# First gated layer of a three-layer network: 18 of its 22 hidden blocks by seven block products instead of eight

## The chip, the cores and the metric

The kernel runs on one core of one Trainium2 chip. The core has a matrix engine (TensorE, PE in the profile), three engines for elementwise work (VectorE or DVE, ScalarE or ACT, GpSimd or POOL), and SyncE (SP), whose queue issues the loads. Each engine works through its own queue in order, and the queues wait for one another on counting semaphores. The metric is the device time of one execution of the whole kernel, in microseconds (us); less is better.

## The reference

The network has two layers with normalised residuals, each a mixer and a gated feed-forward part, and a third layer of another kind with modulated norms. The part that is changed is the gated part of layer 0, on x of 1024 tokens by 1024 features with 2816 hidden features:

```python
def swiglu(x, w_gate, w_up, w_down):
    return (jax.nn.silu(x @ w_gate) * (x @ w_up)) @ w_down
...
        x = layer_norm(DN_ALPHA * x + swiglu(x, ffn_w_gate[layer], ffn_w_up[layer], ffn_w_down[layer]),
                       ffn_ln_g[layer], ffn_ln_b[layer])
```

Beside it lies a product that belongs to the third layer, 24 rows at a time: silu of a condition times the rows of `w_ada`, one number for each feature (`modulation`).

## The kernel before

**Layout.** Features lie on the 128 partitions: x is eight blocks (`DB`) of 128 features by 1024 tokens (`S`); `HALF` is 512 tokens. Hidden features come in 22 blocks (`FFB`) of 128. A PSUM tile `ps0` to `ps3` holds 128 x 1024 f32, two banks of 512 columns.

**Products in three passes.** Each f32 product is made of three matmuls: every operand is split into a high and a low part, and high x high, high x low and low x high are added up in PSUM. x is split into `xh` and `xl` by the norm before, a hidden block into `hh` and `hl`. A weight unit (128 x 1024 f32, 512 KB) is loaded by SP into one of two buffers `stage`, split by ACT into `whi` (`split_hi`, line 178) and by DVE into `wlo` (`split_lo`, line 185), and then used by PE (`mm_unit`, line 202). The next unit for a buffer is loaded once its split is done.

**The gated stage of layer 0.** The hidden blocks go in three groups, 0 to 7, 8 to 14 and 15 to 21. The first four blocks are done by token halves while the norm before is still at work (`Hidden`, `early_act`, `early_dve`, `early_pe`). All others are pairs of a gate unit and an up unit with 48 matmuls each (8 feature blocks x 3 passes x 2 token halves): ACT takes the silu of the gate's PSUM (line 1138), DVE multiplies with the up's PSUM (line 1153), ACT and DVE split the product (lines 1141, 1155). After each of the first two groups comes its down product of eight units, whose PSUM is added to x by `residual` (line 531), with three `modulation`s to every two units (lines 1176, 1178). These rows come in the two buffers `ada`.

**The tail.** The third group's down product is done by token halves, `d0a` then `d0b`, eight units each of 7 x 3 matmuls. DVE evicts a half with `residual_half` (line 526); behind it the sums of the norm `fn0` are made: ACT squares (line 377), POOL adds x and the squares (lines 387, 397), PE totals and broadcasts (lines 408, 455), DVE normalises the first half while the second is still multiplied (lines 475, 477), POOL splits off `xl` (line 494).

**Scratch.** `at_kb(name, shape, kb)` places a tensor at a fixed place in one region of SBUF; `hh`, `hl` and the buffers of later stages share places at different times. The order of the work is written out by hand for each engine; there is no scheduler.

## Time and profile before

| what | value |
|---|---|
| median of 3 runs | 3602.02 us |
| lowest and highest | 3600.16 and 3602.89 us |
| profiled execution, span on the core | 3599.7 us |
| median above that span | 2.3 us |
| busy share of the span | PE 98%, DVE 50%, ACT 34%, POOL 15% |
| gated stage of layer 0, pairs and two down products | 446 to 1006 us |
| its tail, `d0a` and `d0b` | 1006 to 1095 us |

The profile page gives the span of one execution on the core; the runs are timed from outside, and their median stands 2.3 us above the span. A busy share is a mean over all stages.

### The profile page before, as it was taken

The page shows a single profiled execution, that of the slowest core. Times are in us where ns is not written, and L with a number is a line of the kernel's source. Part 1 is how long each engine was busy: PE and PEld are TensorE (multiplying, and loading weights), DVE is VectorE, ACT ScalarE, POOL GpSimd, SP SyncE. Part 2 cuts the span into 40 slices and gives each one's busy share as a digit, 9 for nine tenths or more (in the row PEclk, how much of TensorE's full clock was granted, in tenths as well). Part 3 has the DMA queues.
Part 4 walks back from the last instruction along what each step waited for, and adds up shares of the span by engine and source line. Part 5 has one row for each costly group of instructions (what it writes and reads, how often), then busy time and mean ns, then how long its engine had stood idle before and what let it go on. Part 6 is the DMA issues. An engine that isn't in the chain of part 4 may idle for free. (4 is left out here: it accounts for less than half of the span.)

```text
span 3599.7 us, 41711 instructions
## 1 busy us (share of the span) xinstructions
PE 3523.2 (98%) x16054; PEld 2827.2 (79%) x16054; DVE 1782.8 (50%) x2319; ACT 1234.6 (34%) x1795; POOL 529.2 (15%) x302
## 2 busy tenths in 40 slices
PE   9999999999999999999999999999999899999998
PEld 7768888888887777767888888888877778888886
DVE  7986423233256666667423233564567774323235
ACT  4444410111144444455311112355454442212133
POOL 0007100000042000013100000253223530000004
PEclk9999999999999999999999999999999999999999
DMA  3102213122122111112213123322231222111113
GB/s 105 40 30 89 94 60 109 47 78 86 47 82 82 48 41 47 41 59 77 88 59 105 52 84 108 93 89 94 97 99 48 76 88 88 53 45 48 47 58 100
DMA packets 77474, 259.12 MB, mean 72 GB/s; under 512 B 10288, under 2 KB 11696, under 8 KB 77360
## 3 DMA queue, kind: packets, MB, share of 16 engines
...
## 5 line engine op out<-in xcount | busy, mean ns | idle before, releaser
L202 PE MATMUL ps<-xh,whi 128*128 128x512 f32 x2712 | 941.8, 393 | 14.2 <-POOL xl L494 8.9
L202 PE MATMUL ps<-xh,wlo 128*128 128x512 f32 x2712 | 934.4, 390 | 0.0
L202 PE MATMUL ps<-xl,whi 128*128 128x512 f32 x2712 | 934.1, 390 | 0.0
L185 DVE TENSOR_TENSOR wlo<-stage,whi 128x1024 fp32r<-128x1024 f32 (+1 forms) x361 | 507.2, 1405 | 477.9 <-ACT whi L178 476.7
L178 ACT ACTIVATE whi<-stage 128x1024 fp32r<-128x1024 f32 (+1 forms) x361 | 377.8, 1046 | 1001.2 <-PE ps L202 973.8
L202 PEld LDWEIGHTS ps<-xh,whi 128*128 128x128 f32 x2712 | 511.1, 189 | 130.0 <-POOL xl L494 9.1
L202 PEld LDWEIGHTS ps<-xh,wlo 128*128 128x128 f32 x2712 | 511.2, 188 | 107.3
L202 PEld LDWEIGHTS ps<-xl,whi 128*128 128x128 f32 x2712 | 511.5, 189 | 105.1
L202 PE MATMUL ps<-hh,whi 128*128 128x512 f32 x1216 | 421.5, 395 | 3.1 <-DVE hl L2938 1.6
L202 PE MATMUL ps<-hl,whi 128*128 128x512 f32 x1216 | 420.3, 394 | 0.0
L202 PE MATMUL ps<-hh,wlo 128*128 128x512 f32 x1216 | 420.3, 394 | 0.0
L202 PEld LDWEIGHTS ps<-hh,whi 128*128 128x128 f32 x1216 | 227.7, 187 | 60.8 <-DVE wlo L185 2.5
L202 PEld LDWEIGHTS ps<-hh,wlo 128*128 128x128 f32 x1216 | 227.6, 187 | 56.1
L202 PEld LDWEIGHTS ps<-hl,whi 128*128 128x128 f32 x1216 | 227.7, 187 | 55.3
L387 POOL TENSOR_TENSOR sum_a<-x 128x512 f32<-128x512 f32 x6 | 7.9, 1312 | 1182.7 <-DVE x L526 1182.7
L1153 DVE TENSOR_TENSOR h_t<-g_t,ps 128x1024 f32<-128x1024 f32 (+1 forms) x36 | 40.2, 1117 | 240.2 <-PE ps L202 240.2
L1141 ACT ACTIVATE hh<-h_t 128x1024 f32 (+1 forms) x36 | 35.2, 977 | 330.5 <-DVE h_t L1153 330.5
L1343 PE MATMUL ps<-xh,whi 128*128 128x512 f32 x336 | 146.9, 437 | 0.6 <-DVE wlo L185 0.6
L531 DVE SCALAR_TENSOR_TENSOR x<-x,ps 128x1024 f32<-128x1024 f32 x32 | 39.1, 1221 | 190.1 <-PE ps L202 190.1
L1343 PE MATMUL ps<-xh,wlo 128*128 128x512 f32 x336 | 132.7, 395 | 0.0
L1343 PE MATMUL ps<-xl,whi 128*128 128x512 f32 x336 | 131.6, 392 | 0.0
L1138 ACT ACTIVATE g_t<-ps 128x1024 f32<-128x1024 f32 (+1 forms) x36 | 34.0, 945 | 249.7 <-PE ps L202 249.7
...
## 6 DMA issues: line engine op xcount, KB each, us to landing
stage<-in_w_ff SPq DMA_DIRECT2D x88, 512.0 KB, 3.5
stage<-in_w_gate SPq DMA_DIRECT2D x59, 512.0 KB, 3.4
stage<-in_w_up SPq DMA_DIRECT2D x59, 512.0 KB, 3.4
stage<-in_w_in SPq DMA_DIRECT2D x50, 512.0 KB, 3.4
ada<-in_w_ada SPq DMA_DIRECT2D x48, 512.0 KB, 3.5
stage<-in_w_qkv SPq DMA_DIRECT2D x43, 512.0 KB, 3.4
...
stage<-in_w_out SPq DMA_DIRECT2D x24, 512.0 KB, 3.4
```

The lines of the kernel that those rows point to most:

```text
L178: act.activation(whi[slot][:, wide(g, k)], stage[slot][:, wide(g, k)], ACT.Copy).then_inc(w_hi, 1)
L185: dve.tensor_tensor(wlo[slot][:, n], stage[slot][:, n], whi[slot][:, n].bitcast(F32), ALU.subtract).then_inc(w_split, 1)
L202: done = pe.matmul(acc[:, h * HALF:(h + 1) * HALF], wt[slot][:, w], xt[:, b, h * HALF:(h + 1) * HALF], start=b == 0 and wt is whi and xt i ...
L387: eng.tensor_tensor(self.sums[:, 0, :], x[:, 0, self.t] if j == 1 else self.sums[:, 0, :], x[:, j, self.t], ALU.add).then_inc(s.n_sum1, 1)
L531: dve.scalar_tensor_tensor(x[:, u, :], x[:, u, :], scale, acc_of(g, u)[:], ALU.mult, ALU.add).then_inc(acc_free, 1)
L1138: act.activation(g_t[:, tokens], acc_of(up, 0)[:, tokens], ACT.Silu).then_inc(acc_free, 1)
L1141: act.activation(both(hh[:, bass.ds(i + off, 1), tokens]), h_t[:, tokens], ACT.Copy).then_inc(hh_ready, 1)
L1153: dve.tensor_tensor(h_t[:, tokens], g_t[:, tokens], acc_of(up, 1)[:, tokens], ALU.mult).then_inc(acc_free, 1)
L1343: done = pe.matmul(acc[:, h * HALF:(h + 1) * HALF], wt[slot][:, b * P:(b + 1) * P], xt[:, b, h * HALF:(h + 1) * HALF], start=b == 0 and wt ...
```

## The change

Eighteen gate and up pairs are computed by the Strassen-Winograd scheme. A pair is read as a 2 x 2 matrix of weight blocks (rows: gate and up; columns: the two halves of the 1024 input features) times a 2 x 2 matrix of x (rows: feature halves, columns: token halves). Written as blocks that is eight products of 4 feature blocks x 3 passes = 12 matmuls of 512 columns; the scheme needs seven, on sums of blocks.

The sums of x are made once: t1, the second token half of features 0 to 511 minus the first (it overwrites that quarter of `xh`/`xl`), and t2, t3, t4, which lie at 0 to 48 KB of the scratch region, where `hh` and `hl` were. t1, t2 and t3 begin on POOL beside the early second half (`cross_first_*`), t1's split and t4 beside the early down units (`cross_t1_*`, `cross_t4_*`, `cross_last_pool`). The sums of weights are made for each pair by POOL, four operations of 512 columns (`weight_sums`). A unit is no longer split whole: ACT and DVE split seven parts of 512 columns (`part_hi`, `part_lo`). The seven products go to three banks in the order a, b, a, c, a, c, a. Between them ACT copies bank a or c out (`snapshot`), DVE adds what comes later (`add_up`), and then silu, product and split follow by token halves.

The order of the stage is new too. The early four blocks get a down product of their own at once (`f_e`, 8 units of 24 matmuls). Then come 18 pairs: six groups of two pairs, each followed by its down product (8 units of 12 matmuls, quarter tiles split by `quad_hi`, `quad_lo`, evicted by `down_out`), and six held pairs, whose hidden blocks are kept in f32 and split at the end for `d0a` and `d0b`, now 18 matmuls a unit. `modulation` runs once in each grouped pair and twice in each group's down product, from one buffer `ada0`. The semaphores are older ones with an offset: `x_in0` to `x_in7` stand for `t_sub`, `t_hi`, `t_lo`, `s_add`, `s_hi_w`, `s_lo`, `s_mm`, `s_snap`, and `xh_ready`, `xl_ready`, `g_ready`, `padded`, `lru_taps`, `lru_m`, `lru_v` for `s_sum`, `s_silu`, `s_h`, `s_hh`, `s_hl`, `dn_mm`, `dn_out`.

The core of the diff:

```diff
+                if layer == 0:
+                    plan["down0_e"] = Product(DB, groups(wd, 0, EARLY))
+                    plan["fast0"] = Product(6 * FAST_GROUPS + 2 * FAST_LAST, pair_of(wg, wu, EARLY))
+                    split_product("down0_2", DB, groups(wd, FFB - FAST_LAST, FFB))
+                    return
...
+    FACTORS = [(quarter(xh, X11), quarter(xl, X11)), (quarter(xh, X21), quarter(xl, X21)), (t2[:, 0], t2[:, 1]),
+               (quarter(xh, X12), quarter(xl, X12)), (t3[:, 0], t3[:, 1]), (quarter(xh, X22), quarter(xl, X22)), (t4h[:], t4l[:])]
...
+    def banks(p):
+        if p % 2 == 0:
+            return half(ps[2], 0), half(ps[2], 1), half(ps[3], 0)
+        return half(ps[3], 1), half(ps[1], 0), half(ps[1], 1)
...
+    def weight_sums(pool, p):
+        u = first_unit(p)
+        gate, up = stage
+        if p == 0:
+            pool.wait_ge(mm_done, gf.base + 2)
+        else:
+            pool.wait_ge(*s_lo.at(split_count(p - 1, 5)))
+        pool.wait_ge(w_landed[1], landed(u))
+        pool.tensor_tensor(w_sum[0][:], half(up, 0), half(up, 1), ALU.add).then_inc(s_add.s, 1)
+        pool.wait_ge(w_landed[0], landed(u))
+        pool.wait_ge(*s_add.at(4 * p + 1))
+        pool.tensor_tensor(w_sum[1][:], w_sum[0][:], half(gate, 0), ALU.subtract).then_inc(s_add.s, 1)
+        pool.tensor_tensor(w_sum[2][:], half(gate, 0), half(up, 0), ALU.subtract).then_inc(s_add.s, 1)
+        pool.wait_ge(*s_add.at(4 * p + 2))
+        pool.wait_ge(*s_lo.at(split_count(p, 3)))
+        pool.tensor_tensor(w_sum[0][:], half(gate, 1), w_sum[1][:], ALU.subtract).then_inc(s_add.s, 1)
...
+    def part_hi(act, p, n):
+        if n in (0, 1, 6):
+            act.wait_ge(w_landed[n // 6], landed(first_unit(p)))
+        else:
+            act.wait_ge(*s_add.at(4 * p + {3: 1, 2: 2, 4: 3, 5: 4}[n]))
+        slot_free(act, p, n)
+        act.activation(slot(whi, n), weight_part(n), ACT.Copy).then_inc(s_hi_w.s, 1)
+    def part_lo(dve, p, n):
+        dve.wait_ge(*s_hi_w.at(split_count(p, n)))
+        dve.tensor_tensor(slot(wlo, n), weight_part(n), slot(whi, n).bitcast(F32), ALU.subtract).then_inc(s_lo.s, 1)
...
+    def weight_part(n):
+        return (half(stage[0], 0), half(stage[0], 1), w_sum[1][:], w_sum[0][:], w_sum[2][:], w_sum[0][:], half(stage[1], 1))[n]
...
+    def snapshot(act, p, k):
+        act.wait_ge(*s_mm.at(7 * p + (1, 3, 4)[k]))
+        if p:
+            if p <= 2 * FAST_GROUPS and k < 2:
+                act.wait_ge(*s_hl.at(2 * p - k))
+            else:
+                act.wait_ge(*s_h.at(2 * p - (0, 1, 1)[k]))
+        act.activation((c11, c12, c22)[k][:], banks(p)[(0, 0, 2)[k]], ACT.Copy).then_inc(s_snap.s, 1)
...
+    def add_up(dve, p, k):
+        a, b, c = banks(p)
+        if k == 0:
+            dve.wait_ge(*s_mm.at(7 * p + 2))
+            dve.wait_ge(*s_snap.at(3 * p + 1))
+            dve.tensor_tensor(c11[:], c11[:], b, ALU.add).then_inc(s_sum.s, 1)
+        elif k == 1:
+            dve.wait_ge(*s_mm.at(7 * p + 5))
+            dve.wait_ge(*s_snap.at(3 * p + 3))
+            dve.tensor_tensor(c22[:], c22[:], a, ALU.add).then_inc(s_sum.s, 1)
+        else:
+            dve.wait_ge(*s_mm.at(7 * p + 6))
+            dve.tensor_tensor(c12[:], c12[:], c, ALU.add).then_inc(s_sum.s, 1)
...
+    def product_of(dve, p, k):
+        held = p - 2 * FAST_GROUPS
+        dst = half(hold[held], k) if held >= 0 else (c11, c12)[k][:]
+        if k:
+            dve.wait_ge(*s_silu.at(2 * p + 2))
+            dve.tensor_tensor(dst, c12[:], c22[:], ALU.mult).then_inc(s_h.s, 1)
+        else:
+            dve.wait_ge(*s_silu.at(2 * p + 1))
+            if p == FAST_PAIRS - 1:
+                dve.wait_ge(mm_done, gf.base + gf.n + 2)
+            else:
+                dve.wait_ge(*s_mm.at(7 * p + 7))
+            dve.tensor_tensor(dst, c11[:], banks(p)[0], ALU.mult).then_inc(s_h.s, 1)
...
+    def down_out(dve, g, u):
+        dve.wait_ge(*dn_mm.at(DB * g + u + 1))
+        dve.tensor_tensor(x[:, u, :], x[:, u, :], down_bank(u)[:], ALU.add).then_inc(dn_out.s, 1)
...
+            residual(dve, f_e, u, ALPHA)
+        for n in range(4):
+            part_lo(dve, 0, n)
+        m = 0
+        for p in range(FAST_PAIRS):
+            final = p == FAST_PAIRS - 1
+            part_lo(dve, p, 4)
+            add_up(dve, p, 0)
+            part_lo(dve, p, 5)
+            part_lo(dve, p, 6)
+            if p < 2 * FAST_GROUPS:
...
+            next_dve(dve, p, 0)
+            add_up(dve, p, 2)
+            next_dve(dve, p, 1)
+            product_of(dve, p, 1)
+            product_of(dve, p, 0)
+            if p < 2 * FAST_GROUPS:
+                hidden_lo(dve, p, 1)
+                hidden_lo(dve, p, 0)
+            next_dve(dve, p, 2)
+            next_dve(dve, p, 3)
+            if ends_group(p):
+                g = p // 2
+                down_out(dve, g, 0)
+                down_out(dve, g, 1)
+                modulation(dve, m, ada0, c_row0)
+                part_lo(dve, p + 1, 0)
+                down_out(dve, g, 2)
+                down_out(dve, g, 3)
+                part_lo(dve, p + 1, 1)
+                modulation(dve, m + 1, ada0, c_row0)
+                m += 2
+                down_out(dve, g, 4)
+                down_out(dve, g, 5)
+                part_lo(dve, p + 1, 2)
+                down_out(dve, g, 6)
+                down_out(dve, g, 7)
+                part_lo(dve, p + 1, 3)
...
+    def fast_pair_pe(pe, p):
+        a, b, c = banks(p)
+        target = (a, b, a, c, a, c, a)
+        opens, closes = (0, 1, 3), (1, 5, 6)
+        if p >= 2:
+            pe.wait_ge(*s_h.at(2 * p - 2))
+            pe.wait_ge(*dn_out.at(DB * min(p // 2, FAST_GROUPS)))
+        if p == 1:
+            pe.wait_ge(acc_free, gf.base + 2)
+        for n in range(7):
+            pe.wait_ge(*s_lo.at(split_count(p, n)))
+            if p == 0 and n in (2, 3, 4, 6):
+                pe.wait_ge(*t_lo.at({2: T2_LO, 4: T3_LO, 3: T1_LO, 6: T4_LO}[n]))
+            if n == 1 and p >= 2:
+                pe.wait_ge(*s_sum.at(3 * (p - 2) + 1))
+            if n == 3 and p >= 2:
+                pe.wait_ge(*s_sum.at(3 * (p - 2) + 3))
+            if n in (2, 4, 5):
+                pe.wait_ge(*s_snap.at(3 * p + {2: 1, 4: 2, 5: 3}[n]))
+            if n == 6:
+                pe.wait_ge(*s_sum.at(3 * p + 2))
+            hi, lo = FACTORS[n]
+            for k in range(HB):
+                w = slice(k * P, (k + 1) * P)
+                for wt, xt in ((whi, hi), (whi, lo), (wlo, hi)):
+                    done = pe.matmul(target[n], slot(wt, n)[:, w], xt[:, k, :], start=n in opens and k == 0 and wt is whi and xt is hi,
+                                     stop=n in closes and k == HB - 1 and wt is wlo, skip_group_check=True)
+            if n == 6 and p == FAST_PAIRS - 1:
+                done.then_inc(mm_done, gf.n)
+            else:
+                done.then_inc(s_mm.s, 1)
+    def down_part(pe, g, u, b, halves):
...
+    def fast_down_pe(pe, g):
+        p = 2 * g + 1
+        pe.wait_ge(*s_hl.at(2 * p))
+        for u in range(2):
+            down_start(pe, g, u)
+            down_part(pe, g, u, 0, (0, 1))
+        pe.wait_ge(*s_hl.at(2 * p + 1))
+        for u in range(2):
+            down_part(pe, g, u, 1, (1,))
+        pe.wait_ge(*s_hl.at(2 * p + 2))
+        for u in range(2):
+            down_part(pe, g, u, 1, (0,)).then_inc(dn_mm.s, 1)
+        for u in range(2, DB):
+            down_start(pe, g, u)
+            down_part(pe, g, u, 0, (0, 1))
+            down_part(pe, g, u, 1, (0, 1)).then_inc(dn_mm.s, 1)
...
+        pe.wait_ge(lam_e, 1)
+        for p in range(FAST_PAIRS):
+            fast_pair_pe(pe, p)
+            if ends_group(p):
+                fast_down_pe(pe, p // 2)
+        for u in range(DB):
+            mm_unit(pe, d0a, 0, u, FAST_LAST, lh_hi, lh_lo,
+                    (lambda b: pe.wait_ge(*held_lo.at(HELD.index((b, 0)) + 1))) if u == 0 else None)
```

How the queues are changed by it, at three places, as the built programs have them:

On DVE, after the last pair of a group, the place is the change from pairs to the down product. Before (first group; `ps0`, `ps1` are the down units' PSUM, `ada0`, `ada1` the two row buffers):

```order
L1155 TENSOR_TENSOR hl_1676<-h_t_1678,hh_1675 128x1024
L218 REGISTER_ALU
L218 COMPARE_AND_BRANCH
L185 TENSOR_TENSOR wlo1<-stage1,whi1 128x1024 [waits w_hi,c_act]
L531 SCALAR_TENSOR_TENSOR x<-x,ps0 128x1024 [waits mm_done]
L1176 ISA h_t_1678,ada_sum<-ada0_1680,c_row_1679 128x1024 [waits ada_in0]
L1176 ISA ada_sum 128x1
L1178 TENSOR_TENSOR mod<-ada_sum,cols 128x1 [waits ada_done]
L1176 ISA h_t_1678,ada_sum<-ada1_1681,c_row_1679 128x1024 [waits ada_in1]
```

After, the end of the first group's down product (`lru_m` is `dn_mm`, `x_in4` is `s_hi_w`):

```order
L1188 TENSOR_TENSOR mod<-ada_sum,cols 128x1 [waits ada_done]
L1516 TENSOR_TENSOR x<-x,ps1 128x1024 [waits lru_m]
L1516 TENSOR_TENSOR x<-x,ps2 128x1024 [waits lru_m]
L1426 TENSOR_TENSOR wlo1<-w_sum1_1704,whi1 128x512 [waits x_in4]
L1516 TENSOR_TENSOR x<-x,ps0 128x1024 [waits lru_m]
L1516 TENSOR_TENSOR x<-x,ps1 128x1024 [waits lru_m]
L1426 TENSOR_TENSOR wlo1<-w_sum0_1703,whi1 128x512 [waits x_in4]
```

Splits of the next pair's parts now stand between the evictions, and the last part's split behind the eight evictions.

On PE, at the same place in the program, the down product's end and the next pair's start. Before:

```order
L202 MATMUL ps1<-hl_1676,whi1 128x512 x2
L202 MATMUL ps1<-hh_1675,wlo1 128x512 x2
L218 REGISTER_ALU
L218 COMPARE_AND_BRANCH
L218 UNCONDITIONAL_BRANCH
L218 ISA
L193 REGISTER_ALU [waits w_split]
L202 MATMUL ps0<-xh,whi0 128x512 [waits acc_free]
L202 MATMUL ps0<-xh,whi0 128x512
```

After, at the end of the first group (`lru_v` is `dn_out`, `x_in5` is `s_lo`, `g_ready` is `s_h`):

```order
L1746 MATMUL ps1<-hh_g_1698,whi1 128x512
L1746 MATMUL ps1<-hl_g_1699,whi1 128x512
L1746 MATMUL ps1<-hh_g_1698,wlo1 128x512
L1733 MATMUL ps2<-xh,whi0 128x512 [waits x_in5,lru_v,g_ready]
L1733 MATMUL ps2<-xl,whi0 128x512
L1733 MATMUL ps2<-xh,wlo0 128x512
```

The first matmul of the pair waited for its own tile's release (`acc_free`) and its split; now it also waits for a count of evictions.

The third place is DVE's entry to the first of the 18 pairs, which has no counterpart before:

```order
L185 TENSOR_TENSOR wlo1<-stage1,whi1 128x1024 [waits w_hi]
L537 SCALAR_TENSOR_TENSOR x<-x,ps0 128x1024 [waits mm_done]
L537 SCALAR_TENSOR_TENSOR x<-x,ps1 128x1024 [waits mm_done]
L1426 TENSOR_TENSOR wlo0<-stage0,whi0 128x512 [waits x_in4] x2
L1426 TENSOR_TENSOR wlo1<-w_sum1_1704,whi1 128x512 [waits x_in4]
L1426 TENSOR_TENSOR wlo1<-w_sum0_1703,whi1 128x512 [waits x_in4]
```

The last two early down units are added to x first (`residual`, line 537 of the changed kernel), and the first pair's parts are split behind them.

## Rows read from the trace of the kernel before

**Rows 1.** The page: its head and first part, busy time of each engine.

```profile
span 3599.7 us, 41711 instructions
...
PE 3523.2 (98%) x16054; PEld 2827.2 (79%) x16054; DVE 1782.8 (50%) x2319; ACT 1234.6 (34%) x1795; POOL 529.2 (15%) x302
```

**Rows 2.** Windows: the gated stage, then the tail's first and second half.

```profile
core 0: us, PE busy (x) PEld busy (x) DVE busy (x) ACT busy (x) POOL busy (x), PEclk, DMA share, GB/s
446.00:1006.00 560.00, 560.00 (x2452) 459.30 (x2451) 155.24 (x180) 89.23 (x89) 0.00 (x0) 1.00 0.22 70
1006.00:1046.00 40.00, 38.93 (x168) 31.04 (x167) 21.08 (x20) 14.68 (x19) 21.24 (x12) 1.00 0.30 85
1046.00:1095.00 49.00, 47.80 (x220) 38.52 (x218) 34.64 (x32) 27.28 (x34) 37.50 (x20) 1.00 0.36 118
```

**Rows 3.** Timeline of DVE: the product of gate and up, one each pair.

```profile
874.58 1.22 DVE L1153 TENSOR_TENSOR h_t<-g_t,ps 128x1024 f32<-128x1024 f32 x1 [7.65 <-PE ps L202]
...
896.34 1.22 DVE L1153 TENSOR_TENSOR h_t<-g_t,ps 128x1024 f32<-128x1024 f32 x1 [7.65 <-PE ps L202]
```

**Rows 4.** Timeline of DVE: evictions of two successive down units, group 0.

```profile
543.66 1.22 DVE L531 SCALAR_TENSOR_TENSOR x<-x,ps 128x1024 f32<-128x1024 f32 x1 [5.56 <-PE ps L202]
...
554.86 1.22 DVE L531 SCALAR_TENSOR_TENSOR x<-x,ps 128x1024 f32<-128x1024 f32 x1 [6.17 <-PE ps L202]
```

**Rows 5.** Timeline of all engines, tail, first half: PE, DVE, POOL.

```profile
1016.07 0.39 PE L202 MATMUL ps<-hh,wlo 128*128 128x512 f32 x1
...
1016.50 0.69 DVE L526 SCALAR_TENSOR_TENSOR x<-x,ps 128x512 f32<-128x512 f32 x1 [3.53 <-PE ps L202]
...
1017.27 1.31 POOL L387 TENSOR_TENSOR sum_a<-x 128x512 f32<-128x512 f32 x1 [619.62 <-DVE x L526]
...
1017.66 2.01 DVE L185 TENSOR_TENSOR wlo<-stage,whi 128x1024 fp32r<-128x1024 f32 x1 [0.47 <-ACT whi L178]
...
1018.54 2.28 POOL L397 TENSOR_TENSOR sum_a<-sq_a,sq_a 128x512 f32<-128x512 f32 x1
...
1021.40 0.69 DVE L526 SCALAR_TENSOR_TENSOR x<-x,ps 128x512 f32<-128x512 f32 x1 [1.74 <-PE ps L202]
```

**Rows 6.** Timeline of POOL, tail, second half: sums and splits for the norm.

```profile
1064.04 1.29 POOL L387 TENSOR_TENSOR sum_a<-sum_a,x 128x512 f32<-128x512 f32 x1 [2.24 <-DVE x L526]
...
1093.19 1.27 POOL L397 TENSOR_TENSOR sum_a<-sum_a,sq_a 128x512 f32<-128x512 f32 x1
```

**Rows 7.** Timeline of PE at the end of the tail.

```profile
1094.61 1.92 PE L408 MATMUL ps<-share,sum_a 128*128 128x2 f32 x16 [1.20 <-POOL sum_a L397]
```

**Rows 8.** Timeline of all engines at the tail's second unit.

```profile
1009.83 0.40 PE L202 MATMUL ps<-hh,wlo 128*128 128x512 f32 x1
1010.01 1.23 DVE L185 TENSOR_TENSOR wlo<-stage,whi 128x1024 fp32r<-128x1024 f32 x1 [0.60 <-ACT whi L178]
...
1011.30 0.50 PE L202 MATMUL ps<-hh,whi 128*128 128x512 f32 x1 [1.07 <-DVE wlo L185]
...
1011.63 0.40 PE L202 MATMUL ps<-hl,whi 128*128 128x512 f32 x1
```

**Rows 9.** Lines by form, whole span: mean ns, then idle time before them.

```profile
L178 ACT ACTIVATE whi<-stage 128x1024 fp32r<-128x1024 f32 x353 | 372.7, 1056 | 984.3 <-PE ps L202 967.8 <-PE ps L1987 9.2 <-DMA stage<-in_w_out 3.5
...
L1176 DVE CUSTOM_DVE_ANT_0 h_t<-ada,c_row 128x1024 f32<-128x1024 f32 x48 | 58.5, 1218 | 0.0
...
L1038 DVE TENSOR_TENSOR hl<-h_t,hh 128x512 fp32r<-128x512 f32 x23 | 17.9, 780 | 1.4 <-ACT hh L1033 1.4
...
L1028 DVE TENSOR_TENSOR h_t<-g_t,ps 128x512 f32<-128x512 f32 x23 | 15.8, 688 | 53.1 <-PE ps L202 53.1
...
L1033 ACT ACTIVATE hh<-h_t 128x512 fp32r<-128x512 f32 x23 | 14.2, 618 | 9.1 <-DVE h_t L1028 9.1
```

**Rows 10.** DMA issues of the page: KB each, us from issue to landing.

```profile
stage<-in_w_gate SPq DMA_DIRECT2D x59, 512.0 KB, 3.4
```

**Rows 11.** Windows: the stretch at half clock; columns as in rows 2.

```profile
1096.90:1100.30 3.40, 3.40 (x14) 2.86 (x12) 0.53 (x4) 0.30 (x1) 0.00 (x0) 0.50 0.64 175
```

More of the change, by code:

```diff
@@ new lines, in part_lo, with quad_hi, quad_lo @@
+    def part_lo(dve, p, n):
+        dve.wait_ge(*s_hi_w.at(split_count(p, n)))
+        dve.tensor_tensor(slot(wlo, n), weight_part(n), slot(whi, n).bitcast(F32), ALU.subtract).then_inc(s_lo.s, 1)
+    def quad_hi(act, g, n):
+        act.wait_ge(w_landed[n // 2], landed(quad_first(g)))
+        act.wait_ge(*s_mm.at(7 * (2 * g + 1) + (5, 6, 7, 4)[n]))
+        act.activation(slot(whi, n), half(stage[n // 2], n % 2), ACT.Copy).then_inc(s_hi_w.s, 1)
+    def quad_lo(dve, g, n):
+        dve.wait_ge(*s_hi_w.at(quad_count(g, n)))
+        dve.tensor_tensor(slot(wlo, n), half(stage[n // 2], n % 2), slot(whi, n).bitcast(F32), ALU.subtract).then_inc(s_lo.s, 1)
@@ new lines, in down_part, with down_start @@
+    def down_part(pe, g, u, b, halves):
+        n = u // 2
+        w = slice((u % 2) * 2 * P + b * P, (u % 2) * 2 * P + (b + 1) * P)
+        for h in halves:
+            for wt, ht in ((whi, hh_g), (whi, hl_g), (wlo, hh_g)):
+                done = pe.matmul(half(down_bank(u), h), slot(wt, n)[:, w], half(ht[:, b, :], h), start=b == 0 and wt is whi and ht is hh_g,
+                                 stop=b == 1 and wt is wlo)
+        return done
+    def down_start(pe, g, u):
+        pe.wait_ge(*s_lo.at(quad_count(g, u // 2)))
+        if u == 1:
+            pe.wait_ge(*s_sum.at(3 * (2 * g + 1) + 3))
+        if u == 2:
+            pe.wait_ge(*s_sum.at(3 * (2 * g) + 3))
+            pe.wait_ge(*s_h.at(2 * (2 * g) + 2))
+        if u > 2:
+            pe.wait_ge(*dn_out.at(DB * g + u - 2))
@@ L2268, in _ @@
             early_pe(pe, f0, *mix0)
[L2269 to L2272 removed]
+            fast_pe(pe)
             mm_unit(pe, gqa, 0, 0, DB, xh, xl, arrived(pe, fn0[0]))
```

332 lines of the change are left out of this document (306 added, 26 removed).

## The prediction

> **What bounds the kernel now.** I read the page first: the matrix engine PE is busy 98% of the span and no other engine over half [rows 1]. The windows say whether that holds where the change is made. From 446 to 1006 us, the first layer's gated stage, they show PE busy without a gap at the full clock, and the other engines at a third or less; in the tail, where the last down product runs by token halves, PE has small gaps, and POOL is the fullest beside it [rows 2]. So within the stage time is matmuls times pitch, and work taken from PE there shortens the span unless a new wait takes its place; in the tail it need not.
>
> **The pitch.** Two DVE evictions of successive gate/up pairs start 21.76 us apart [rows 3]. A pair is 96 matmuls of 512 columns (8 blocks x 3 passes x 2 halves x 2 weights), so 226.7 ns each. Two evictions of successive down units start 11.20 us apart [rows 4]; 48 matmuls, 233.3 ns each. The first streams `xh`/`xl`, the second tensors in the lower scratch region (`hh`, `hl`).
>
> **Term 1, seven products for eight.** A pair becomes 7 x 12 = 84 matmuls: 18 x 12 = 216 fewer, at 226.7 ns: -49.0 us.
>
> **Term 2, where the factors lie.** Three of the seven products stream t2, t3 and t4, which lie where `hh` lay. If the pitch of [rows 4] belongs to the place, 18 x 36 = 648 matmuls cost 6.7 ns more: +4.3. If it belongs to down units, 0. I take +4.3, the nearest row by place, and keep 0. The Trainium skill ("TensorE: Matmul & The Clock Gate", section "Wait — 56ns, not 53.3ns?") gives 215.7 ns for back-to-back 512-column matmuls at full clock, and knows no place; by it term 1 would be -46.6 and this one 0, a net of -46.6 where the rows give -44.7. The rows differ from it and decide.
>
> **Term 3, the down products.** Their matmuls stay 22 x 48 = 1056 (192 after the early blocks, 6 x 96 in groups, 288 in the tail): 0 by count. But 48 of them leave the tail, where PE is not the only bound, for the stage, where they cost all of 233.3 ns (11.2 us). The d0a units are 4.90 us apart, 21 matmuls [rows 5]; with 18 they take 4.20, so the first half gives back 8 x 0.7 = 5.6 us. In the second half POOL waits 2.24 us for unit 1's residual and then runs without a break from 1064.04 until 1094.46, where PE's total of the norm waits for it [rows 6, 7]. Units 0 and 1 ending 0.7 us earlier each start that chain 1.4 us earlier; the other 4.2 us are not given back: +4.2. Bounds: 5.6 if the chain doesn't move, 0 if it closes up.
>
> **Term 4, six group openings.** Product 0 of pairs 2, 4, 6, 8, 10 and 12 waits for all eight `down_out`s of the group before. The last one starts 0.20 us after the pitch of the last matmul ends (matmul at 1016.07, eviction at 1016.50, less 0.233) [rows 5], takes 1.22 for 1024 columns with one input in PSUM [rows 4], PE follows 0.06 after a DVE end (10.01 + 1.23 to 11.30), and the next matmul comes 0.33 instead of 0.23 us after the first (1011.30 to 1011.63), +0.1 [rows 8]. 1.58 x 6 = +9.5. Nothing covers it: the queue of PE is in order, and the whole next pair stands behind the wait. As written the wait can't be shorter than that; it is longer if DVE is late with units 5 and 6 or has a split ahead, up to 0.7 more each, +4.
>
> **Term 5, entry to the first pair.** DVE has `residual` of the last early unit ahead of `part_lo(0,0)` in its queue, and PE needs the latter: 0.20 + 1.22 + 0.69 (a 512-column operation of DVE: L1028, and L1038 with 0.78 [rows 9]) + 0.06 + 0.1 = +2.3; 1.5 if the split comes first after all, 2.9 if POOL's sums slow it as they slow a split in [rows 5].
>
> **Term 6, a smaller one.** At the second unit of the tail PE now stalls 1.24 + 0.1 us for a `wlo` [rows 8]. After the change, behind the last product's end, ACT has four pieces of 0.6 (held blocks) and the unit's `whi` of 1.06, and DVE its `wlo` of 1.22 [rows 9]: ready after 5.0 to 5.2 with the handovers, wanted after 18 matmuls, 4.2. A stall of about 1.0 in place of 1.35: -0.4.
>
> **What I cost at nothing, and its cover.** A pair lasts 48 x 0.2267 + 36 x 0.2333 = 19.28 us. Per pair DVE has 7 `part_lo`, 2 `hidden_lo` and a product from SBUF at 0.69 to 0.78, 4 evictions from PSUM at 0.69 and a modulation of 1.22: 10.9 to 11.8 us. ACT has 14 pieces of about 0.62, 8.7 us. POOL has 4 sums at 1.31, 5.2 us [rows 5, 9]. The tightest need is `add_up` of index 1 before product 6: it follows product 4's end (13.8 us into the pair) by under 1.0, PE wants it at 16.5. Product 2 wants its split at 5.4, ready by about 3.5. POOL's sums follow the landing of the two units (512 KB, 3.4 us [rows 10]): split of part 6 near 8 us, landed by 11.5, three sums by 15.4, and the first of them is wanted 5.4 us into the next pair, some 9 us later. Within a down group a unit lasts 2.8 us, while DVE does one `down_out` (1.22) and at most half a modulation and half a split, 2.3 in all. The cross sums ride beside the early hidden half and beside the early down units, which last 5.6 us and ask DVE for 1.22 + 1.22 + 2 x 0.69 = 3.8: 0, at most 3. The adaLN rows (512 KB each, as the units) now go through one buffer instead of two; each is asked for at least 4.8 us after the row before it was used: 0.
>
> **The sum.** -49.0 + 4.3 + 4.2 + 9.5 + 2.3 - 0.4 = -29.1. The profiled execution's span is 3599.7, so 3570.6; the median stands 2.3 above that span [rows 1], so 3573.
>
> **Rival a: POOL and DVE slow each other and a pair runs late.** The trace has the effect. Where POOL runs, its 512-column square sum takes 2.28 us where the one before took 1.31, and DVE's split of 1024 columns 2.01 where it took 1.23 before POOL began, while the eviction with a PSUM input stays at 0.69 [rows 5, 8]. In the stage before, POOL is at zero [rows 2], so this is new there. If every sum takes 2.28 (9.1 us) and DVE's ten pieces from SBUF wait for POOL instead of running beside it, DVE's 10.9 + 9.1 = 20.0 us pass the 19.3 of a pair by 0.7 us, and a piece behind a sum is late more than this mean. One us in each pair is +18: 3591. Against it: the margins above are 2 us and more, and only about half the pair has sums in it. The Trainium skill ("SBUF — State Buffer", section "🎯 Summary: rules for kernel authors") says that when DVE has two SBUF inputs while a GpSimd operation reads SBUF, the second one to issue blocks until the first is through; the durations in [rows 5, 8] agree.
>
> **Rival b: the place costs nothing and the tail closes up.** Term 2 and most of term 3 go: 3573 - 4.3 - 4.2 = 3564.5. For it: nothing in the trace moves `xh` into that region or `hh` out of it.
>
> **Rival c: the opening waits drop the clock.** PE fell to half its clock, 1.2 GHz, from 1096.9 to 1100.3 after it had waited for POOL at 1094.6 and worked in sixteen 2-column matmuls [rows 7, 11]; a stretch of 3.4 us at half clock does 1.7 us of work, so it loses 1.7. Seven such drops: +12, 3585. Against it: the 1.24 us stall at 1011.30 did not lower the clock, which is 1.00 over the whole window around it [rows 2, 8].
>
> **Rival d, slower than before: the weight sums' ring becomes the bound.** One pair of stages serves a pair's loads, sums and splits, and the next loads start only when parts 5 and 6 are split. The ring: load 3.4, four sums, splits of parts 5 and 6 (each 0.62 on ACT and 0.69 on DVE), with queueing behind ACT's snapshots about 1.5: 12.8 us when nothing contends; with 2.28 for each sum and 1.3 for each split about 18 to 19. PE's pair is 19.28, so the ring is hidden unless it grows further; it undoes the gain at 19.28 + 29.1/18 = 20.9 us and is 0.2% slower at 21.3, 3609. That needs more than 2 us a pair beyond full contention.
>
> **Numbers.** A change under 0.2% (7 us) can hardly be told from none here. The forecast holds with 0.58; a 0.20 (3580 to 3602, of which a sixth is within 0.2%), b 0.10, c 0.06, d 0.06 (half of it within 0.2%, 3595 to 3609, half beyond). So faster 0.90, same 0.06, slower 0.04. The forecast's own range is 3567 to 3579, from its bounds (term 2 down to 0, term 3 between 0 and 5.6, openings and cross sums up by 4). The range with b, c and the lower half of a: 3562 to 3591.
>
> **What would show it.** In the profile after: evictions of successive held pairs 19.3 us apart with PE busy throughout (rival a and d: PE idle before L1733, released by DVE's `wlo` or by POOL); matmuls on t2, t3, t4 233 ns apart (b: 227); six PE waits of about 1.5 us released by DVE `x` L1516; one of about 2.2 at the first pair; d0a units 4.2 us apart, d0b units still over 5; granted clock 1.00 throughout the stage (c: 0.50 after an opening). I am wrong if waits inside the pairs sum to over 10 us, or if the openings cost much more or less than 1.6 each.

## The result, and the profile after

| | before | after |
|---|---|---|
| median, 4 runs each | 3602.45 us | 3579.44 us |
| lowest and highest | 3600.16 to 3604.06 | 3578.83 to 3580.70 |
| span of the profiled execution | 3599.7 | 3577.7 |

The changed kernel is faster: ratio 0.994, 95% interval 0.9928 to 0.9953, 23.0 us by the medians and 22.0 by the spans. The forecast was 3573, with a range of its own of 3567 to 3579 and one with the rivals of 3562 to 3591: the time lies 0.4 us above the first and inside the second.

The page of the changed kernel, to be set beside [rows 1]:

```profile
span 3577.7 us, 41727 instructions
...
PE 3481.6 (97%) x15838; PEld 2784.3 (78%) x15838; DVE 1966.8 (55%) x2572; ACT 1327.5 (37%) x2008; POOL 669.0 (19%) x398
```

PE has 216 matmuls fewer, and its busy time fell by more than the span; it is now idle for 96.1 us of the span, 76.5 before.

Windows of the gated stage, of the two halves of the tail and of a stretch in the early down units, with the columns of [rows 2] (the number after the five engines is the granted clock):

```profile
446.00:989.00 543.00, 530.56 (x2281) 427.20 (x2280) 327.59 (x421) 178.39 (x293) 124.11 (x84) 1.00 0.24 75
989.00:1028.00 39.00, 38.30 (x164) 30.25 (x162) 25.33 (x25) 16.00 (x21) 24.60 (x14) 1.00 0.32 92
1028.00:1071.00 43.00, 38.57 (x175) 30.47 (x174) 31.94 (x30) 25.52 (x32) 33.93 (x19) 1.00 0.38 120
475.60:479.30 3.70, 3.55 (x9) 2.79 (x10) 0.50 (x2) 1.05 (x2) 2.52 (x2) 0.54 0.24 73
```

The stage was without a gap before; now PE is idle for 12.4 us in it, and in the 3.7 us from 475.6 the mean granted clock is 0.54, for most of them half, 1.2 GHz.

**Pairs.** Timeline of DVE, the last product of two successive held pairs:

```profile
931.37 0.69 DVE L1503 TENSOR_TENSOR hold<-fast_c,ps 128x512 f32<-128x512 f32 x1 [0.16 <-PE ps L1733]
...
950.71 0.69 DVE L1503 TENSOR_TENSOR hold<-fast_c,ps 128x512 f32<-128x512 f32 x1
```

19.34 us, where the pairs before had 21.76 [rows 3]. Timeline of PE in one of them: first matmul of a product on t2, of the next on xh, of the next on t3 (a row with x2 holds two matmuls):

```profile
917.22 0.63 PE L1733 MATMUL ps<-t,whi 128*128 128x512 f32 x2
...
920.02 0.39 PE L1733 MATMUL ps<-xh,whi 128*128 128x512 f32 x1
...
922.76 0.63 PE L1733 MATMUL ps<-t,whi 128*128 128x512 f32 x2
```

Twelve matmuls on t2 take 2.80 us (233.3 ns each), twelve on xh behind them 2.74. No pair of this kernel shows a wait inside it.

**Openings.** Timeline of all engines where the first group ends and pair 2 begins:

```profile
557.86 0.40 PE L1746 MATMUL ps<-hh_g,wlo 128*128 128x512 f32 x1
558.29 1.22 DVE L1516 TENSOR_TENSOR x<-x,ps 128x1024 f32<-128x1024 f32 x1 [1.58 <-PE ps L1746]
...
559.62 0.47 PE L1733 MATMUL ps<-xh,whi 128*128 128x512 f32 x1 [1.36 <-issue]
...
559.92 0.40 PE L1733 MATMUL ps<-xl,whi 128*128 128x512 f32 x1
```

PE's last down matmul starts at 557.86, DVE evicts unit 7 from 558.29 to 559.51, and PE goes on at 559.62. (The page names "issue" as what ended the wait; the end of the eviction is 0.11 us ahead of it.) All six openings have this gap of 1.76 us from matmul to matmul, and 0.31 behind it.

**Entry.** Timeline of all engines at the first pair: the last early eviction, and the matmul behind it:

```profile
494.88 1.22 DVE L537 SCALAR_TENSOR_TENSOR x<-x,ps 128x1024 f32<-128x1024 f32 x1 [4.38 <-PE ps L202]
...
496.91 0.47 PE L1733 MATMUL ps<-xh,whi 128*128 128x512 f32 x1 [2.08 <-DVE wlo L1426]
```

**A stall that was not forecast.** Timeline of all engines in the early down units. `t_f`, `t_c` and `t_d` are raw sums for t1 and t4, `t4h`, `t4l` the parts of t4, `wlo` the low weights of down unit 5:

```profile
467.15 0.69 DVE L1371 TENSOR_TENSOR xl<-t_f,xh 128x512 fp32r<-128x512 f32 x1
...
467.92 1.31 POOL L1358 TENSOR_TENSOR t_c<-xh,t 128x512 f32<-128x512 f32 x1 [14.93 <-DVE xl L1371]
...
470.56 1.29 POOL L1361 TENSOR_TENSOR t_c<-t_c,t_d 128x512 f32<-128x512 f32 x1
...
471.89 0.63 ACT L1377 ACTIVATE t4h<-t_c 128x512 fp32r<-128x512 f32 x1 [7.64 <-POOL t_c L1361]
...
472.55 0.69 DVE L1382 TENSOR_TENSOR t4l<-t_c,t4h 128x512 fp32r<-128x512 f32 x1 [4.71 <-ACT t4h L1377]
...
473.16 1.21 DVE L537 SCALAR_TENSOR_TENSOR x<-x,ps 128x1024 f32<-128x1024 f32 x1
...
474.29 1.40 DVE L185 TENSOR_TENSOR wlo<-stage,whi 128x1024 fp32r<-128x1024 f32 x1
...
475.75 1.16 PE L202 MATMUL ps<-hh_e,whi 128*128 128x512 f32 x2 [1.98 <-DVE wlo L185]
```

PE wanted unit 5 at 473.6 and got it at 475.75. Read upwards: `wlo` stood in DVE's queue behind an eviction (473.16) and `t4l` (472.55), for which DVE had been idle for 4.71 us; `t4l` waited for `t4h` on ACT, which waited for POOL's third sum, and POOL began its three sums only at 467.92, after the last split of t1. The high part of the unit's weights was late as well, behind `t4h` in ACT's queue (472.43 to 473.47), but done 0.8 us before DVE came to `wlo`.

**The tail.** Timeline of DVE, evictions of two d0a units, 4.20 us apart (4.90 before, [rows 5]):

```profile
998.68 0.69 DVE L532 SCALAR_TENSOR_TENSOR x<-x,ps 128x512 f32<-128x512 f32 x1 [2.78 <-PE ps L202]
...
1002.88 0.69 DVE L532 SCALAR_TENSOR_TENSOR x<-x,ps 128x512 f32<-128x512 f32 x1 [0.98 <-PE ps L202]
```

Timeline of POOL in the second half, first and last operation of a chain without a break (16 operations):

```profile
1040.82 2.40 POOL L393 TENSOR_TENSOR sum_a<-sum_a,x 128x512 f32<-128x512 f32 x1 [1.90 <-DVE x L532]
...
1070.17 1.26 POOL L403 TENSOR_TENSOR sum_a<-sum_a,sq_f 128x512 f32<-128x512 f32 x1
```

1040.82 to 1071.43 is 30.6 us; before it was 30.4 [rows 6]. Timeline of all engines in it, a DVE split beside POOL, and PE's wait for it:

```profile
1050.84 2.95 DVE L185 TENSOR_TENSOR wlo<-stage,whi 128x1024 fp32r<-128x1024 f32 x1
...
1053.84 0.73 PE L202 MATMUL ps<-lh,whi 128*128 128x512 f32 x2 [1.38 <-DVE wlo L185]
```

And PE at the norm's total, which waited 1.94 us for POOL, 1.20 before [rows 7]:

```profile
1071.58 2.09 PE L414 MATMUL ps<-share,sum_a 128*128 128x2 f32 x16 [1.94 <-POOL sum_a L403]
```

**POOL beside DVE.** Timeline of POOL and DVE in one held pair: a sum, a split of a part that begins during it, and a split with no sum beside it:

```profile
925.76 1.31 POOL L1394 TENSOR_TENSOR w_sum<-stage 128x512 f32<-128x512 f32 x1 [10.34 <-DMA stage<-in_w_up]
926.48 1.14 DVE L1426 TENSOR_TENSOR wlo<-stage,whi 128x512 fp32r<-128x512 f32 x1
...
940.71 0.69 DVE L1426 TENSOR_TENSOR wlo<-stage,whi 128x512 fp32r<-128x512 f32 x1 [2.53 <-ACT whi L1421]
```

POOL and DVE hold each other up, as rival a said. The split that begins during the sum ends 0.55 us behind the sum's end, 1.14 us for 0.69. Of the 126 splits at this line 40 begin during a sum; the 33 of them that begin over 0.2 us before its end all end 0.55 us behind it, so each waits for what is left of the sum. In the pairs it cost PE nothing.

### The profile page after: what moved, and what is told of

Read it like the earlier page. It is cut to its first block and busy times, and to the rows that moved or that the text cites. A ratio compares the mean times of both kernels' runs of the same rounds, so it can differ in the third digit from the quotient of the medians.

```text
span 3577.7 us, 41727 instructions
## 1 busy us (share of the span) xinstructions
PE 3481.6 (97%) x15838; PEld 2784.3 (78%) x15838; DVE 1966.8 (55%) x2572; ACT 1327.5 (37%) x2008; POOL 669.0 (19%) x398
## 5 line engine op out<-in xcount | busy, mean ns | idle before, releaser
L202 PE MATMUL ps<-xl,whi 128*128 128x512 f32 x2136 | 756.7, 391 | 0.0
L202 PE MATMUL ps<-xh,wlo 128*128 128x512 f32 x2136 | 756.5, 391 | 0.0
L202 PEld LDWEIGHTS ps<-xh,whi 128*128 128x128 f32 x2136 | 402.8, 189 | 108.4 <-POOL xl L500 9.8
L202 PEld LDWEIGHTS ps<-xh,wlo 128*128 128x128 f32 x2136 | 403.0, 189 | 85.0
L202 PEld LDWEIGHTS ps<-xl,whi 128*128 128x128 f32 x2136 | 403.4, 189 | 82.8
L202 PE MATMUL ps<-hh,whi 128*128 128x512 f32 x864 | 301.4, 395 | 2.1 <-DVE hl L3514 1.7
L202 PE MATMUL ps<-hh,wlo 128*128 128x512 f32 x864 | 300.9, 394 | 0.0
L202 PE MATMUL ps<-hl,whi 128*128 128x512 f32 x864 | 300.8, 394 | 0.0
L202 PEld LDWEIGHTS ps<-hh,whi 128*128 128x128 f32 x864 | 161.8, 187 | 42.7 <-issue 2.1
L202 PEld LDWEIGHTS ps<-hh,wlo 128*128 128x128 f32 x864 | 161.7, 187 | 39.9
L1924 PE MATMUL ps<-xh,wlo 128*128 128x512 f32 x336 | 132.7, 395 | 0.0
L1924 PE MATMUL ps<-xl,whi 128*128 128x512 f32 x336 | 131.8, 392 | 0.0
```

Source lines behind the costliest of these rows:

```text
L202: done = pe.matmul(acc[:, h * HALF:(h + 1) * HALF], wt[slot][:, w], xt[:, b, h * HALF:(h + 1) * HALF], start=b == 0 and wt is whi and xt i ...
L1924: done = pe.matmul(acc[:, h * HALF:(h + 1) * HALF], wt[slot][:, b * P:(b + 1) * P], xt[:, b, h * HALF:(h + 1) * HALF], start=b == 0 and wt ...
```

## Experiments

Stages are told by the starts of matmuls: **early down** from the first down matmul of the early blocks to the first pair (51.5 us in the changed kernel), **pairs** from there to the tail's first matmul (492.2), **tail** from there to the first product of the next layer (74.9).

### The wait at the openings

```diff
-            pe.wait_ge(*dn_out.at(DB * min(p // 2, FAST_GROUPS)))
+            pe.wait_ge(*dn_out.at(DB * min(p // 2, FAST_GROUPS) - (2 if p % 2 == 0 else 0)))
```

> Product 0 of an opening pair waits only for the eviction of down unit 5, the last that used its bank; the next, odd pair waits for all eight. Theory 1 (the six openings cost PE 1.61 us each because the wait covers banks the product does not touch): the six gaps of 1.76 us become 0.23, the two waits move to places where they are long satisfied, the span falls by 9.7 us, to 3568 against 3577.7 (time near 3570). Rival (something else is as late there, the split of part 0 or 2 behind the evictions on DVE): the gap stays over 1 us or comes back at product 2, and the span falls by less than 4 us.

Measured: 3572.11 us (3571.49 to 3573.35), ratio to before 0.9921, interval 0.9904 to 0.9937; span 3569.7. Timeline of all engines at the same place:

```profile
557.43 0.39 PE L1746 MATMUL ps<-hh_g,wlo 128*128 128x512 f32 x1
...
557.66 0.39 PE L1733 MATMUL ps<-xh,whi 128*128 128x512 f32 x1
...
557.86 1.22 DVE L1516 TENSOR_TENSOR x<-x,ps 128x1024 f32<-128x1024 f32 x1 [1.58 <-PE ps L1746]
```

The pair follows the down unit after 0.23 us, and the eviction of unit 7 runs beside it. Pairs fell from 492.2 to 482.6 us, 9.6 less. Of this 1.5 came back in the tail, where the clock fell for a stretch in which the changed kernel had kept it (windows, the stretch):

```profile
1021.40:1024.80 3.40, 3.40 (x10) 2.61 (x9) 0.18 (x1) 0.03 (x1) 0.00 (x0) 0.51 0.42 120
```

Theory 1 holds for the openings; the rival is out.

### The early down units

```diff
-            if 2 <= u < 2 + HB:
-                cross_t4_act(act, u - 2)
+            if 3 <= u < 3 + HB:
+                cross_t4_act(act, u - 3)
```

(the same for `cross_t4_dve`)

> The splits of t4 on ACT and DVE stand one early down unit later in both queues (units 3 to 6 instead of 2 to 5). Theory 1 (the 2.15 us stall of PE at 475.75 us is the order of the queues: ACT and DVE wait in line for a sum that POOL begins only after the last split of t1, and the weight split behind them is late; the half clock after it, 1.7 us, is its consequence): stall and clock drop go, the span falls by about 4.4 us. Rival (POOL's chain of three sums, a split on each side and the next sums is simply longer than a down unit of 5.6 us): the stall moves one or two units on, and the span falls by under 2 us.

Measured: 3575.46 us (3571.93 to 3579.58), ratio 0.9927, interval 0.9911 to 0.9944; span 3575.9. Early down fell from 51.5 to 47.3 us: stall and half clock are gone there. But the clock fell a little later, at the entry wait, which had not lowered it in the changed kernel. Timeline of PE:

```profile
491.94 0.74 PE L1733 MATMUL ps<-xh,whi 128*128 128x512 f32 x1 [2.06 <-DVE wlo L1426]
492.47 0.63 PE L1733 MATMUL ps<-xl,whi 128*128 128x512 f32 x1
492.90 0.63 PE L1733 MATMUL ps<-xh,wlo 128*128 128x512 f32 x1
```

0.43 us from one matmul to the next is half speed. Pairs and tail grew by 1.6 and 1.5. The four runs' spans are 3575.9 (the one profiled), 3571.3, 3577.8 and 3570.2 us, at mean granted clocks of 0.986, 0.989, 0.987 and 0.989, so the clock may have fallen less often in two of them, which no trace shows. The order of the queues made the stall, as theory 1 says; that the clock's fall belongs to this stall alone is refuted.

### The entry

```diff
+            if u == DB - 1:
+                part_lo(dve, 0, 0)
+                part_lo(dve, 0, 1)
             residual(dve, f_e, u, ALPHA)
-        for n in range(4):
+        for n in range(2, 4):
             part_lo(dve, 0, n)
```

> DVE splits parts 0 and 1 of the first pair before it adds the last early down unit to x, not after. Theory 1 (the 2.23 us wait at the first pair is the eviction ahead of the split in DVE's queue): the gap of 2.46 us at 496.9 becomes 0.23 and the span falls by 2.3 us. Rival (ACT's half of the split is as late): a wait of about 1 us stays.

Measured: 3579.67 us (3577.68 to 3579.82), ratio 0.9939, interval 0.9922 to 0.9955; span 3577.9. Timeline of all engines at the entry:

```profile
494.56 0.63 PE L202 MATMUL ps<-hh_e,wlo 128*128 128x512 f32 x2
...
495.03 0.39 PE L1736 MATMUL ps<-xh,whi 128*128 128x512 f32 x1
```

The wait is gone (early down 49.3, 2.2 less). The time did not move, since the tail grew by 1.5 to a half clock at 1029.6 and the rest, behind the first attention scores, by 0.9.

### The three together

> The three edits together: narrower wait at the group openings, t4 one down unit later, parts 0 and 1 of the first pair ahead of the last early eviction. Theory 1 (each of the three waits is on the path by itself): early down products 45.0 us (from 51.5), pairs 482.6 (from 492.2), no half clock before the tail; span 3577.7 - 9.6 - 4.3 - 2.2 = 3561.6, plus up to 3 where the clock falls in the tail: time 3563 to 3567. Rival (part of each gain is given back to another wait or to the clock): over 3570.

Measured: 3565.43 us (3563.75 to 3565.68), ratio 0.9899, interval 0.9882 to 0.9915; span 3563.5. Early down 45.0, pairs 482.5, tail 76.3. Windows of the stage and of the one stretch at half clock in its tail:

```profile
446.00:976.00 530.00, 530.00 (x2295) 429.30 (x2294) 325.93 (x426) 180.83 (x298) 122.40 (x84) 1.00 0.25 78
1015.30:1018.70 3.40, 3.40 (x10) 2.63 (x9) 0.18 (x1) 0.00 (x0) 0.00 (x0) 0.51 0.40 115
```

The stage is without a gap again. The three waits were each on the path, and add: 16.2 us less in early down and pairs, of which 1.4 came back in the tail.

### POOL's work doubled

```diff
+        pool.tensor_tensor(w_sum[0][:], half(up, 0), half(up, 1), ALU.add).then_inc(s_add.s, 1)
+        pool.wait_ge(*s_add.at(8 * p + 1))
         pool.tensor_tensor(w_sum[0][:], half(up, 0), half(up, 1), ALU.add).then_inc(s_add.s, 1)
```

(so for all four sums, with the counts doubled)

> Every weight sum is made twice on POOL, each time with the same result: 8 operations a pair instead of 4, 11.8 us instead of 5.9 by the measured means. Forecast (cover inside the pair; ring of load, sums and splits 12.8 + 5.9 = 18.7 us, against a pair of 19.3): pairs stay within 1 us of 19.34, the span grows by 0 to 18 us. Rival a (POOL's time adds to DVE's, 12 + 12 = 24 us in a pair of 19.3): each pair grows by 4 us or more, the span by 70 us or more.

Measured: one run, 3591.10 us, span 3589.3. Pairs grew by 11.1 us in all, but not evenly: the first by 4.8 and the second by 0.5, the twelve behind them by 1.6 together, and the last four, which follow one another without a down product between, by 0.3, 1.0, 1.1 and 1.8. Timeline of PE, the largest wait and that of the last pair:

```profile
510.35 0.70 PE L1741 MATMUL ps<-t,whi 128*128 128x512 f32 x2 [2.46 <-ACT fast_c L1470]
...
990.63 0.70 PE L1741 MATMUL ps<-t,whi 128*128 128x512 f32 x2 [1.03 <-ACT fast_c L1470]
```

Both are for ACT's snapshot, which stands behind the split of part 5 and so behind POOL's fourth sum; the first was followed by a half clock. Rival a as it was priced, 24 us in a pair, is out. Rival d is not out at twice the sums: the last pair took 21.16 us (19.34 in the changed kernel), over the 20.9 that d names, and whether a longer row of pairs would grow further no run shows.

### The tail without POOL's sums

```diff
+            if self.squares is sq_f and j > 1:
+                a, b, c = a[:, 0:16], b[:, 0:16], c[:, 0:16]
```

> In the tail the sums of the first layer's last norm are cut to 16 columns from the second block on (the norm is then wrong), so that POOL has nearly nothing to do for them; POOL's splits stay. Theory 1 (POOL's chain bounds the tail's second half and keeps back what the shorter down units give): the two PE waits of 1.55 us at 1053.8 and 1059.7 and the 2.1 us before the norm's total go, tail and total together 4 to 6 us shorter. Rival (DVE's queue, 4.35 us a unit and more beside POOL, is the bound): the waits stay over 1 us, under 2 us in all are gained.

Measured: one run, 3576.16 us, span 3574.4. The tail fell by 2.9 us and the stretch behind it, up to the first attention scores, by 1.5: 4.4. The wait at the norm's total is gone, and of the two for `wlo` in the second half one is left, 0.80 us for 1.38 (timeline of PE):

```profile
1056.99 0.73 PE L202 MATMUL ps<-lh,whi 128*128 128x512 f32 x2 [0.80 <-DVE wlo L185]
```

So POOL's sums keep back what the shorter units give. Whether they do it by the length of POOL's own chain or by holding up DVE's splits, this run doesn't tell apart: it shortens both. In the changed kernel the two splits that held PE began during POOL's split of `xl` (line 500), which this run leaves in, and ended 1.08 us behind it; the sums ahead of it set when it runs.

### Why t2, t3, t4 and the hidden blocks stream at 233 ns

```diff
-    sd = sb("sd", [P, 2, 1])
-    rstd = sb("rstd", [P, 2, 1])
```

> Two small unused tiles are taken out, so that the scratch region begins 64 bytes lower, at a multiple of 1024 bytes instead of 64 above a multiple of 128; nothing else differs. Theory 1 (the 233 ns of matmuls that stream from that region come from the region's byte address, as xh at a multiple of 128 has 227): t2, t3, t4 and the hidden blocks run at 227 ns or less, in this layer's stage 648 + 1056 matmuls x 6.6 ns = 11 us, in the whole kernel some 4000 x 6.6 = 25 us at most. Rival (the pitch depends on what the matmul sequence is, or on the distance to the weights, not on the address): 233 ns stays and the span is unchanged within 1 us.

Measured: 3578.20 us (3577.98 to 3581.45), ratio 0.9939, interval 0.9923 to 0.9956. Timeline of PE, first matmul on t2 and on the xh product behind it:

```profile
916.92 0.62 PE L1731 MATMUL ps<-t,whi 128*128 128x512 f32 x2
...
919.71 0.39 PE L1731 MATMUL ps<-xh,whi 128*128 128x512 f32 x1
```

2.79 us for 2.80. The rival seemed right, but single matmuls no longer took 233 ns: behind a first two of 234 and 224 they alternated between 238 and 229, 232.7 in the mean of the twelve.

```diff
-    xl = sb("xl", [P, DB, S], F32R)
+    xl = nc.alloc_sbuf_tensor_at("xl", [P, DB, S], F32R, offset=196480)
```

(with the edit before it)

> xl moves to the top of the buffer (byte 196480), the scratch region moves down to 109568, and xh stays at 49280; all at multiples of 128 bytes. Theory 1 (the upper part of a partition, above some 128 KB, streams at 233 ns and the lower at 227): matmuls on xl take 233 ns, t2 at 109568 takes 227 (-6 ns), hh_g at 158720 stays 233; with 216 x 4 of xl's in this stage and a third of all products elsewhere the span grows by 10 to 20 us. Rival (the pitch depends on something else, such as the distance between the weights and the streamed tensor, or the shape of the tensor): xl stays at 227 and t2 at 233.

Measured: one run, 3581.98 us, span 3580.2. Timeline of PE, products on t2 (now in the lower part), on xh with xl (now at the top), and the next:

```profile
648.88 0.62 PE L1731 MATMUL ps<-t,whi 128*128 128x512 f32 x2
...
651.67 0.39 PE L1731 MATMUL ps<-xh,whi 128*128 128x512 f32 x1
...
654.40 0.62 PE L1731 MATMUL ps<-t,whi 128*128 128x512 f32 x2
```

2.79 us for t2 at byte 109568, 2.73 for the product with xl at 196480, as in the run before: theory 1 is out. What the two runs share is the address modulo 256: 0 for the region, 128 for xh, xl and the weights. In the changed kernel the region is at 64.

```diff
+    mv = sb("mv", [P, 2, 2])
+    stats = sb("stats", [P, 2, 2, 6])
+    sd = sb("sd", [P, 2, 1])
+    rstd = sb("rstd", [P, 2, 1])
     x = sb("x", [P, DB, S])
```

(moved up from behind the weights)

> x, xh, xl, the weight buffers and the splits all begin 192 bytes higher, at 64 above a multiple of 256, as the scratch region already does; the region stays. Theory 1 (a streamed tensor's own byte address, modulo 256, sets the pitch: 227 ns at 128, 233 at 64 and 0): xh and xl go to 233 ns, the span grows by some 60 us. Theory 2 (what counts is the streamed tensor's address against the weights' address, modulo 256): xh stays at 227 and t2, t3, t4 and the hidden blocks come down to 227; the span falls by 15 to 25 us. Rival (address has nothing to do with it): no pitch changes.

Measured: one run, 3551.49 us, span 3549.7. Timeline of PE, t2 and the xh product behind it:

```profile
907.72 0.62 PE L1733 MATMUL ps<-t,whi 128*128 128x512 f32 x2
...
910.44 0.39 PE L1733 MATMUL ps<-xh,whi 128*128 128x512 f32 x1
```

2.72 us, 226.7 ns each, on t2; xh has the same, and so has the region, which did not move. Theory 1, the tensor's own address, is out; theory 2, the distance to the weights, fits. The run moved x, xh, xl, the raw weights and the split ones together; that the split weights, which PE reads beside the streamed tensor, are what counts is the likely reading and not shown apart. The span fell by 28.0 us, more than the 15 to 25 expected. The other way to distance 0, the region moved:

```diff
-    one = sb("one", [P, 1])
+    trio = sb("trio", [P, 4])
+    one, share, eps = trio[:, 0:1], trio[:, 1:3], trio[:, 3:4]
...
+    quad = sb("quad", [P, 4, 2, 2])
+    mx, nb, den, rden = [quad[:, k] for k in range(4)]
+    pad = sb("pad", [P, 8])
```

> Small tiles are packed so that the scratch region begins 192 bytes lower, at 128 above a multiple of 256, like xh and the weights; all else as in the changed kernel. Theories 1 and 2 alike: t2, t3, t4 and the hidden blocks at 227 ns: in this stage 648 + 1056 matmuls x 6.6 ns, 11 us, some 7 more in the second layer's down products, more in the third layer where PE bounds it: the span 3577.7 falls by 15 to 25 us. Rival (the address modulo 256 has nothing to do with it): 233 ns stays, within 1 us of 3577.7.

Measured: 3556.11 us (3553.34 to 3558.74), ratio 0.9877, interval 0.9862 to 0.9893; span 3551.6. The other three runs had spans of 3552.3 to 3557.0, so the fall from 3577.7 is 21 to 26 us. t2, t3, t4 and the hidden blocks of this layer and the later ones all run at 227 ns: 648 matmuls and 3 x 1216, whose pitch before is that of [rows 4], at 6.6 ns each 28.4 us. In the profiled run 7.3 us of the gain are in the pairs and groups, 17.9 behind the first attention scores, in the later layers.

> The three shorter waits together with the region at 128 above a multiple of 256. The two gains touch different things, so they should add: span 3563.5 - 15 to 25 us, time near 3545 by theories 1 and 2; 3565 by the rival.

Measured: 3536.64 us (3536.14 to 3537.70), ratio 0.9821, interval 0.9808 to 0.9835; span 3534.9: 43 us under the changed kernel, 65 under the one before (3601.48 in the same session), and 8 under the 3545 expected. The two gains add, 14.2 and 26.1 us of span to 42.8; the 2.5 above their sum come with a clock that fell neither at the entry nor in the tail's first half, as it did in e10.

```diff
-    t2 = at_kb("t2", [P, 2, HB, HALF], 0, F32R)
-    t3 = at_kb("t3", [P, 2, HB, HALF], 16, F32R)
-    t4h = at_kb("t4h", [P, HB, HALF], 32, F32R)
+    t2 = at_kb("t2", [P, 2, HB, HALF], 0 + 32 / KB, F32R)
+    t3 = at_kb("t3", [P, 2, HB, HALF], 16 + 64 / KB, F32R)
+    t4h = at_kb("t4h", [P, HB, HALF], 32 + 224 / KB, F32R)
```

(and their neighbours by 224 or 256)

> As the kernel with shorter waits and the region at 128 above a multiple of 256, but t2 begins 32 bytes, t3 64 bytes and t4 224 bytes past that place, modulo 256, counted from the weights; hh_g, hl_g and xh stay at distance 0. So far: distance 0 gave 227 ns, 192 (64 below) 233, 128 between 224 and 238 with a mean near 233. Theory 2 (only the distance to the weights modulo 256 counts, and 0 is best): xh and hh_g stay at 227, the three t products come to 229 to 238, the span grows by 2 to 6 us over 3534.9. Rival (0 is not special, and another distance lets a matmul of 512 columns go faster): one of the three is under 226.

Measured: one run, 3542.40 us, span 3540.6, 5.7 more than the kernel it was made from. Timeline of PE, products on xh, on t4 and on xh:

```profile
905.02 0.40 PE L1731 MATMUL ps<-xh,whi 128*128 128x512 f32 x1
...
907.79 0.40 PE L1731 MATMUL ps<-t4h,whi 128*128 128x512 f32 x1
...
910.59 0.39 PE L1731 MATMUL ps<-xh,whi 128*128 128x512 f32 x1
```

Over all pairs t2 (distance 32) has 233.6 ns, t3 (64) 230.3 and t4 (224) 233.5; xh right behind them 229 to 231. None is under 226.7.

## Why the forecast came out as it did

| term | forecast | measured |
|---|---|---|
| 1, seven products for eight | -49.0 | -49.0 by count and pitch, +1.1 as a pair is 19.34, not 19.28 |
| 2, t products | +4.3 | +4.3 (2.80 us a product) |
| 3 and 6, the tail | +3.8 | +4.1 |
| 4, six openings | +9.5 | +9.7 |
| 5, entry | +2.3 | +2.3 |
| early down units | 0, at most 3 | +4.4 |
| sum | -29.1 | -23.1 |

The spans fell by 22.0; the 1.1 between that and the sum lies outside these terms, 1.0 of it behind the first attention scores. **Terms 1 and 2** were right in size. The 1.1 us are the matmuls just behind a change from one pitch to the other. The cause that term 2 left open, place or kind of unit, is settled by the last six runs: it is neither the region as such nor the down units, but the byte distance modulo 256 from the weights to the streamed tensor. (x, xh and xl stood at the weights' place modulo 256 in all runs, so that it is the weights is not shown apart.) The 215.7 ns that the Trainium skill gives ("TensorE: Matmul & The Clock Gate", section "Wait — 56ns, not 53.3ns?") is in no run here; 226.7 is the best that these rows show for this stream of matmuls.

**Term 3** was right in mechanism: the first half gave back its 5.6 us and the second mostly not. From the tail's first matmul to the next layer's first product there were 82.7 us before and 74.9 after, 7.8 less of 11.2, and 0.7 of it was lost again before the norm's total. Run e8 shows POOL's sums as the cause, directly or through DVE's splits. The forecast did not see that DVE's splits, 2.95 us beside POOL, would hold PE twice for 1.55 us on the way.

**Terms 4 and 5** came to the tenth, from four durations each. Runs e1 and e3 show that the eviction is what was waited for, in the first by itself and in the second as what stands ahead of the split. That term 4 could not be under its price held only "as written": the bank that product 0 uses was free two units earlier.

**What failed** is a step in "what I cost at nothing": the cross sums in the early down units. I compared DVE's own work, 3.8 us, with a unit's 5.6. What counted was a chain through three queues: the second block of t4's sums counts on all four splits of t1, then come three sums on POOL (3.9 us), ACT's and DVE's split of t4, and behind the latter in DVE's queue an eviction and the next unit's weight split. It cost 2.15 us of waiting, 1.65 at half clock and 0.5 at the next unit; the bound of 3 was too low by the clock. This is most of the 6.0 us by which the sum missed. That the time still lies in the wide range is owed to the lower half of rival a, whose mechanism took nothing from PE in the pairs: so far it is luck. The range of its own was also drawn tighter than the bounds that it names: 1.4 more for term 3, 4 for the openings and 3 for the cross sums make 3581.

**Rival a** had the effect right and the price wrong: the two engines slow each other, but the pairs from the second to the fifteenth had room for twice the sums, 6.6 us more of POOL's work, at under 0.5 us each (e7). The whole blocking that was cited beside it is what the single splits show: each that met more than the last 0.2 us of a sum ended 0.55 us behind it. It adds up to little in a pair, as a split waits only for what is left of a sum and 86 of the 126 meet none; the price took all of POOL's time on top of DVE's. In the tail, where POOL has no break, a split takes 2.95 us for 1.22. **Rival c** named the wrong wait: six openings of 1.53 us did not lower the clock, one stall of 2.15 did. It cost 1.65 us, once, where 1.7 were worked out. **Rivals b and d** did not occur in the changed kernel; how near d is, the last pairs of e7 show.
